# Twelve-layer fp32 network on one core: gate and up products under one 512-column operand, stage ends in token halves

## The chip, the cores and the metric

The kernel runs on one core of a Trainium2 chip. The metric is the device time of one execution in microseconds (us); the median of three runs before the change is 2283.48 us.

## The reference

Two networks follow each other on x of 256 tokens by 1024 features, all in float32. Each layer is a mixer or an FFN between two RMS norms:

```python
x = x + _rms(m, g[1])                                    # m: conv, pool or attention mixer of _rms(x, g[0])
f = _swiglu(_rms(x, g[2]), ffn_w_gate[i], ffn_w_up[i], ffn_w_down[i])
x = x + _rms(f, g[3])
def _swiglu(xn, w_gate, w_up, w_down):
    return (jax.nn.silu(xn @ w_gate) * (xn @ w_up)) @ w_down
```

There are eight FFNs with a hidden width of 2816, two convolution mixers, one pooling mixer, one differential attention and two mixers of dilated attention beside an mLSTM: 14 stages, in the order conv, ffn, pool, ffn, attn, ffn, conv, ffn, ffn, mix, ffn, ffn, mix, ffn.

## The kernel before

**Products.** Every float32 product is made of three products of parts in the type float32r: high times high, high times low, low times high (`three`, L483 to L487). Weights arrive in units of 1 MB (128 partitions by 2048 values), 349 in all, by the queue of SyncE into a ring of six buffers `raw`. ScalarE (ACT) copies a unit to its high part `w_hi` (L954, ring of four), VectorE (DVE) subtracts to get the low part `w_lo` (L1284, ring of six, in the place of `raw`). ACT may overwrite a high part once the unit four before is used (`unit_used`), and SyncE issues a load once the unit six before is used. `split(u)` is this step on ACT and on DVE, and `advance(to)` does all splits below `to` that are not done yet; its place in an engine's program sets when the split is made, since each engine works its list in order.

**An FFN stage** has 33 units: 11 steps of a gate unit, an up unit (256 hidden columns each) and an output unit. A gate or up unit is a `feature_unit`: the weights are stationary, the normed rows, transposed and split (`xT_hi`, `xT_lo`, 256 tokens), move, 48 matmuls of 256 columns. The first two units of a stage are made in token halves instead (`token_half`: 24 matmuls of 256 columns for 128 tokens, the rows stationary and the weights moving), so that half 0 can start before half 1 is normed; their product is turned by four transposes (`product_columns`). ACT applies Silu, DVE multiplies (`h_full`), ACT and DVE split the product into `h_hi` and `h_lo`, and the output unit adds 24 matmuls of 512 columns to four PSUM banks, two per token half. Steps 2 to 9 run in a hardware loop of two turns on each engine. The last two output units of a stage are ordered so that half 0 is finished first (`last_units`).

**A stage end** (the main loop over stages in the scalar and vector programs) is, for each token half h: squares of the sums (ACT, L982), 1/rms (POOL, L1764 to L1769), Y = sums times gain (DVE, L1725), X = Y * rstd + X (DVE, L1738), squares of X (ACT, L982), 1/rms (POOL), Y = X times gain (DVE, L1300), then times rstd (DVE, L1304), eight transposes on TensorE (`transpose_rows`, L576), the high part by ACT (`transposed`), the low part by DVE (L1312). Half 1's transposes stand after the first token half of the next stage (`first_units`). ACT and DVE do the splits up to unit `end` + 1 (`advance(end + 2)`, `end` is the first unit of the next stage) before the stage end begins. At the end of stage 0, DVE also copies `bias_row`, and POOL then writes it to DRAM 128 times over (L1847).

Of the kernel before, what the change touches and what calls it, by code (L numbers as in the profile page):

```python
# [38 lines left out]
HI_RING = 4  # L39
FFN_STEPS = FF // W  # L40
LOOP_STEPS = 4
TURNS = (FFN_STEPS - 3) // LOOP_STEPS
TURN = 3 * LOOP_STEPS
# [114 lines left out]
def build(nc, a, tab_at, tables, out, only=None):  # L158
# [25 lines left out]
    with ctx:  # L184
# [14 lines left out]
        xT_hi = sb("xT_hi", [P, KC, S], F32R)  # L199
        xT_lo = sb("xT_lo", [P, KC, S], F32R)  # L200
# [14 lines left out]
        with ExitStack() as g:  # L215
# [9 lines left out]
            bias_row = sb("bias_row", [4, 2 * S], scope=g)  # L225
        with ExitStack() as g:
# [111 lines left out]
        in_read = sem("in_read")  # L338
        gate_ready = sem("gate_ready")
        prod_ready = sem("prod_ready")  # L340
# [53 lines left out]
        def _(sp):  # L394
            def load(u, source, it=None):

                if u >= LO_RING:
                    v = u - LO_RING + 1
                    sp.wait_ge(unit_used, v if it is None else it * TURN + v)
                dst = raw[u % LO_RING][:].rearrange("p (c n) -> p c n", c=source.shape[1])  # L400
                sp.dma_start(dst, source).then_inc(raw_loaded[u % LO_RING], 16)
# [16 lines left out]
            for st in stages:  # L418
                u = st["u0"]
                if st["kind"] == "ffn":  # L420
                    w_gate, w_up, w_down, up0 = ffn_sources(st)

                    def block_in(u, i, it=None):

                        for n, (w, c) in enumerate(((w_gate, 0), (w_up, up0))):
                            c0 = c + i * W
                            c0 = c0 if it is None else it * (LOOP_STEPS * W) + c0
                            load(u + n, w[:, :, bass.ds(c0, W)], it)

                    def block_out(u, i, it=None):  # L430
                        r0 = i * W if it is None else it * (LOOP_STEPS * W) + i * W
                        load(u, chunks(w_down[bass.ds(r0, W), :]), it)
# [3 lines left out]
                    block_out(u + 4, 0)  # L436
                    with sp.Fori(0, TURNS) as it:
                        for b in range(LOOP_STEPS):
                            block_in(u + 5 + 3 * b, 2 + b, it)
                            block_out(u + 7 + 3 * b, 1 + b, it)  # L440
                    block_in(u + 29, FFN_STEPS - 1)
                    block_out(u + 31, FFN_STEPS - 2)
                    block_out(u + 32, FFN_STEPS - 1)
                elif st["kind"] == "conv":
                    ia = st["layer"] // 3
                    w_in, w_out = chunks(a["conv_w_in"][ia]), a["conv_w_out"][ia]
                    for i in range(D // W):
# [5 lines left out]
                        if i:  # L453
                            load(u, chunks(w_out[(i - 1) * W:i * W, :]))
                            u += 1
                    load(u, chunks(w_out[D - W:, :]))
# [23 lines left out]
        def _(pe):  # L480
# [8 lines left out]
            def unit_there(u, k, it=None):  # L489

                pe.wait_ge(lo_ready, u + 1 if it is None else it * TURN + (u + 1))
                return [w.rearrange("p (k n) -> p k n", k=k) for w in (w_hi[u % HI_RING][:], w_lo[u % LO_RING][:])]

            def feature_unit(u, b, it=None):
                hi, lo = unit_there(u, KC, it)
# [7 lines left out]
            def token_half(u, b, h):  # L503
# [3 lines left out]
                for k in range(KC):  # L507
                    mm = three(pair(b)[:, h, :], xT_hi[:, k, rows], xT_lo[:, k, rows],
# [26 lines left out]
            def product_columns():  # L535

                pe.wait_ge(prod_ready, seen.next(prod_ready))
                for c in range(2):
                    for h in range(H):
                        mm = pe.transpose(pair(4)[:, c, h * P:(h + 1) * P], prod[:, h, c * P:(c + 1) * P], ident[:])  # L540
                mm.then_inc(prodT_done, 1)

            def out_half(u, x_hi, x_lo, h, first, last, it=None):

                hi, lo = unit_there(u, 2, it)
# [11 lines left out]
            def out_unit(u, x_hi, x_lo, first, it=None):  # L557
                out_half(u, x_hi, x_lo, 0, first, False, it)
                out_half(u, x_hi, x_lo, 1, first, False, it).then_inc(unit_used, 1)

            def last_units(u, xs, before_last=None):

                out_half(u, *xs[0], 0, False, False)
                if before_last is not None:
                    pe.wait_ge(before_last, seen.next(before_last))
                out_half(u + 1, *xs[1], 0, False, True).then_inc(acc_done, 1)
                out_half(u, *xs[0], 1, False, False).then_inc(unit_used, 1)
                out_half(u + 1, *xs[1], 1, False, True).then_inc(unit_used, 1)

            def transpose_rows(h):  # L570

                for b in range(2):
                    pe.wait_ge(xn_ready, seen.next(xn_ready))
                    for j in range(4):
                        k = 4 * b + j
                        mm = pe.transpose(bank(4 + 2 * h + b)[:, j * P:(j + 1) * P],  # L576
# [3 lines left out]
            def ffn(u):  # L580
                base = seen.now(h_ready)

                def step_in(u, i, it=None):
                    for n in range(2):
                        feature_unit(u + n, 4 + 2 * (i % 2) + n, it)

                def step_out(u, i, it=None):
# [1294 lines left out]
```

## Time and profile before

| | |
|---|---|
| timed runs, median of 3 | 2283.48 us (2283.34 to 2283.98) |
| profiled execution, from its first to its last instruction | 2282.2 us |
| TensorE busy | 2183.5 us (96%), 15124 matmuls |
| VectorE busy | 1277.5 us (56%) |
| ScalarE busy | 992.4 us (43%) |
| mean granted clock of TensorE | 0.980 |

The page gives no time of the profiled execution other than this span. A busy time counts an instruction from its start to its end, overlaps only once; matmuls are pipelined, so the distance between two starts, not the duration of one, tells what one costs in a stream.

### The profile page before, as it was taken

To read this page: it belongs to the slowest core of one execution; us is meant where nothing else is said; L and a number is where in the kernel's file an instruction comes from. 1 tells how busy PE (TensorE), PEld (TensorE's weight loads), DVE (VectorE), ACT (ScalarE), POOL (GpSimd) and SP (SyncE) were. 2 spreads that over 40 slices of the span, in tenths; PEclk is the share of its full clock that TensorE was granted. 3 is DMA by queue.
4 is the path that set the end of the run, shared out by engine and by line. 5 is a ranking of instruction groups with operands and counts; after the bars stand their busy time and mean duration, and the time that the engine had idled before them with its cause. 6 is when DMAs were issued, how large, how long until landed. Compare 5 with 4: busy or idle time off the path is not lost.

```text
span 2282.2 us, 35632 instructions
## 1 busy us (share of the span) xinstructions
PE 2183.5 (96%) x15124; PEld 2027.6 (89%) x15124; DVE 1277.5 (56%) x1340; ACT 992.4 (43%) x1074; POOL 118.0 (5%) x231
## 2 busy tenths in 40 slices
PE   7969988999989999999999999989999999998998
PEld 7869978998979998899989989879998998887998
DVE  5645455445565457645464556775455545777454
ACT  4433444434554344344343444654344334455433
POOL 0000011001010000100020010010002001001000
PEclk9989999999999999999999999999999999999999
DMA  7556546555446555555565553236556555424552
GB/s 253 185 142 213 187 158 183 185 184 185 148 134 199 184 185 183 177 176 185 185 215 186 185 184 125 88 122 199 184 184 217 185 184 166 130 75 157 185 184 92
DMA packets 288662, 392.43 MB, mean 172 GB/s; under 512 B 7512, under 2 KB 255112, under 8 KB 288416
## 3 DMA queue, kind: packets, MB, share of 16 engines
q1 hardware_dynamic: 280928, 368.21, 49.6%
q10 hardware_dynamic: 4032, 14.68, 2.0%
q0 software_dynamic: 3584, 7.84, 1.6%
q8 instruction: 89, 1.46, 0.3%
q14 instruction: 29, 0.24, 0.0%
HBM read 388.60 MB, written 2.10 MB: 171 GB/s over the span
## 4 chain that ended last, share of the span: by engine, by line
PE 88%; DVE 5%; DMA 2%; ACT 2%; POOL 2%; issue 1%; POOLq 0%; DVEq 0%; SPq 0%; ACTq 0%
PE psum L485 28%; PE psum L487 27%; PE psum L486 27%; DMA raw<-in_ffn_w_up 2%; ACT squares L982 1%; POOL mean L1764 1%; DVE w_lo L1284 1%; DVE Y L1725 1%; DVE xT_lo L1312 1%; POOL rstd L1769 1%; DVE Y L1304 1%; DVE X L1738 1%; PE psum L841 1%; PE psum L869 1%; PE psum L576 1%
## 5 line engine op out<-in xcount | busy, mean ns | idle before, releaser
L485 PE MATMUL psum<-xT_hi,w_hi 128*128 128x256 f32 x3264 | 931.8, 285 | 16.2 <-DVE w_lo L1284 14.9
L486 PE MATMUL psum<-xT_lo,w_hi 128*128 128x256 f32 x3264 | 926.1, 284 | 0.0
L487 PE MATMUL psum<-xT_hi,w_lo 128*128 128x256 f32 x3264 | 925.9, 284 | 0.0
L1284 DVE TENSOR_TENSOR w_lo<-raw,w_hi 128x2048 fp32r<-128x2048 f32 x349 | 784.9, 2288 | 206.4 <-ACT w_hi L954 205.8
L954 ACT ACTIVATE w_hi<-raw 128x2048 fp32r<-128x2048 f32 x349 | 656.9, 1907 | 76.2 <-PE psum L487 46.2
L485 PEld LDWEIGHTS psum<-xT_hi,w_hi 128*128 128x128 f32 x3264 | 623.9, 191 | 26.0 <-DVE w_lo L1284 15.1
L486 PEld LDWEIGHTS psum<-xT_lo,w_hi 128*128 128x128 f32 x3264 | 623.9, 191 | 4.4 <-issue 1.0
L487 PEld LDWEIGHTS psum<-xT_hi,w_lo 128*128 128x128 f32 x3264 | 623.9, 191 | 0.0
L1347 DVE TENSOR_TENSOR h_full<-gate,psum 128x512 f32<-128x512 f32 x80 | 55.1, 688 | 471.1 <-PE psum L487 471.1
L487 PE MATMUL psum<-w_hi,h_lo 128*128 128x512 f32 x768 | 302.0, 393 | 0.0
L485 PE MATMUL psum<-w_hi,h_hi 128*128 128x512 f32 x768 | 300.3, 391 | 0.0
L486 PE MATMUL psum<-w_lo,h_hi 128*128 128x512 f32 x768 | 299.9, 391 | 0.0
L954 ACT ACTIVATE h_hi<-h_full 128x512 fp32r<-128x512 f32 x88 | 55.6, 632 | 493.8 <-DVE h_full L1347 441.9
L485 PE MATMUL psum<-w_hi,xT_hi 128*128 128x256 f32 (+1 forms) x688 | 219.3, 319 | 36.3 <-DVE xT_lo L1312 23.8
L486 PE MATMUL psum<-w_lo,xT_hi 128*128 128x256 f32 (+1 forms) x688 | 213.3, 310 | 0.0
L487 PE MATMUL psum<-w_hi,xT_lo 128*128 128x256 f32 (+1 forms) x688 | 212.8, 309 | 0.0
L485 PEld LDWEIGHTS psum<-w_hi,xT_hi 128*128 128x128 f32 x688 | 139.7, 203 | 50.1 <-DVE xT_lo L1312 26.7
L1003 ACT ACTIVATE gate<-psum 128x512 f32<-128x512 f32 x88 | 52.5, 596 | 292.1 <-PE psum L487 292.1
L487 PEld LDWEIGHTS psum<-w_hi,h_lo 128*128 128x128 f32 x768 | 144.3, 188 | 31.2
L486 PEld LDWEIGHTS psum<-w_lo,h_hi 128*128 128x128 f32 x768 | 144.2, 188 | 29.4
L485 PEld LDWEIGHTS psum<-w_hi,h_hi 128*128 128x128 f32 x768 | 144.4, 188 | 27.5
L487 PEld LDWEIGHTS psum<-w_hi,xT_lo 128*128 128x128 f32 x688 | 139.9, 203 | 4.1
(214 smaller groups left out, 1341.3 us busy)
## 6 DMA issues: line engine op xcount, KB each, us to landing
raw<-in_ffn_w_in SPq DMA_DIRECT2D x88, 1024.0 KB, 5.1
raw<-in_ffn_w_gate SPq DMA_DIRECT2D x44, 1024.0 KB, 5.3
raw<-in_ffn_w_up SPq DMA_DIRECT2D x44, 1024.0 KB, 5.3
raw<-in_ffn_w_down SPq DMA_DIRECT2D x44, 1024.0 KB, 4.9
raw<-in_ffn_w_out SPq DMA_DIRECT2D x44, 1024.0 KB, 4.9
raw<-in_mix_w_in SPq DMA_DIRECT2D x28, 1024.0 KB, 5.3
raw<-in_conv_w_in SPq DMA_DIRECT2D x24, 1024.0 KB, 5.2
raw<-in_attn_w_qkv SPq DMA_DIRECT2D x12, 1024.0 KB, 5.2
```

The lines of the kernel that those rows point to most:

```text
L485: pe.matmul(dst, l_hi, r_hi, start=first, stop=False, skip_group_check=loose)
L486: pe.matmul(dst, l_hi, r_lo, start=False, stop=False, skip_group_check=loose)
L487: return pe.matmul(dst, l_lo, r_hi, start=False, stop=last, skip_group_check=loose)
L576: mm = pe.transpose(bank(4 + 2 * h + b)[:, j * P:(j + 1) * P], Y[:, h, k * P:(k + 1) * P], ident[:])
L841: mm = pe.matmul(pair(0)[:, h, :], aqk[r, hd // 2, h * P:(h + 1) * P], aqk[r, 4 + hd // 2, :], start=True, stop=True)
L869: mm = pe.matmul(psum[r0:r0 + 64, 2 if hd < 6 else 5, 0:S], av[:, k, hd * 64:(hd + 1) * 64], a_probT[hd % 2][:, k, :], start=k == 0, stop= ...
L954: return act.activation(dst, source, ACT.Copy, **kw)
L982: act.activation(squares[:, 0:source.shape[1]], source, ACT.Square, scale=1.0 / 32, accum_out=ssum[:, col:col + 1]).then_inc(ss_ready, 1)
L1003: act.activation(gate[:], pair(4 + 2 * (i % 2)), ACT.Silu).then_inc(gate_ready, 1)
L1284: dve.tensor_tensor(w_lo[u % LO_RING][:], raw[u % LO_RING][:], f32(w_hi[u % HI_RING][:]), ALU.subtract).then_inc(lo_ready, 1)
L1304: dve.tensor_scalar(Y[:, h, c], Y[:, h, c], rstd[:, 2 + h:3 + h], None, ALU.mult).then_inc(xn_ready, 1)
L1347: dve.tensor_tensor(h_full[:], gate[:], pair(5 + 2 * (i % 2)), ALU.mult).then_inc(full_ready, 1)
```

## The change

1. `xT_hi` and `xT_lo` lie side by side in one tensor `xT`. In steps 2 to 10 of an FFN a gate or up unit is a `stacked_unit`: for each weight block, the high part meets high and low rows at once (512 columns, one whole PSUM bank), the low part meets the high rows (256 columns, added to the first half of the bank). The sum of the bank's two halves is the result: ACT copies the low half to SBUF, DVE adds the high half.
2. Steps 0 and 1 of an FFN are both in token halves, four units, each product turned by transposes. The output unit of step i stands after the gate and up units of step i + 2; the last three output units of an FFN, and of a convolution, are made half 0 first. There are four buffers of `h_hi` and `h_lo` instead of two. The hardware loops are gone.
3. The normed rows are made in one pass, from X, rstd and gain. Transposes go to PSUM banks 0 to 3, half 0's are served before half 1's sums, and a first product waits for half of the rows at a time.
4. The splits at a stage end stand elsewhere: `advance(end + 1)` ahead of it, the next after half 0, and two more within half 1.

```diff
+            def stacked_unit(u, b):
+                hi, lo = unit_there(u, KC)
+                for c in range(2):
+                    cols = slice(c * P, (c + 1) * P)
+                    for k in range(KC):
+                        pe.matmul(pair(b + c), hi[:, k, cols], xT[:, k, :, :], start=k == 0, stop=False)
+                        mm = pe.matmul(pair(b + c)[:, 0, :], lo[:, k, cols], xT_hi[:, k, :],
+                                       start=False, stop=k == KC - 1)
+                mm.then_inc(unit_used, 1)
...
             def first_units(u, b):
-                pe.wait_ge(xt_ready, seen.next(xt_ready, 2))
-                token_half(u, b, 0)
+                token_half(u, b, 0, rows_come=True)
+                token_half(u + 1, b + 1, 0)
                 transpose_rows(1)
-                token_half(u + 1, b + 1, 0)
-                pe.wait_ge(xt_ready, seen.next(xt_ready, 2))
-                token_half(u, b, 1).then_inc(unit_used, 1)
+                token_half(u, b, 1, rows_come=True).then_inc(unit_used, 1)
                 token_half(u + 1, b + 1, 1).then_inc(unit_used, 1)
...
+            def last_units(u, xs, made=None):
+                last = len(xs) - 1
+                for h in range(H):
+                    for n, x in enumerate(xs):
+                        if made is not None and h == 0:
+                            pe.wait_ge(made, seen.next(made))
+                        mm = out_half(u + n, *x, h, False, n == last)
...
             def ffn(u):                                   # TensorE
+                for n, b in enumerate((6, 7, 4, 5)):
+                    if n == 3:
+                        transpose_rows(1)
+                    token_half(u + n, b, 0, rows_come=n == 0)
+                for n, b in enumerate((6, 7, 4, 5)):
+                    if n == 3:
+                        pe.wait_ge(gate_taken, seen.next(gate_taken))
+                        product_columns(0)
+                    token_half(u + n, b, 1, rows_come=n == 0).then_inc(unit_used, 1)
+                for i in range(2, FFN_STEPS):
+                    step_in(u + 3 * i - 2, i)             # two stacked units, banks 6, 7 and 4, 5
+                    if i < FFN_STEPS - 1:
+                        step_out(u + 3 * i, i - 2)
+                last_units(u + 30, [(h_hi[i % H_BUFFERS], h_lo[i % H_BUFFERS])
+                                    for i in range(FFN_STEPS - 3, FFN_STEPS)], h_ready)
...
             def ffn(st):                                  # VectorE, steps 2 to 10
+                    dve.wait_ge(gate_low, seen.next(gate_low))
+                    dve.tensor_tensor(gate[:], psum[:, 6:8, 0:S], gate[:], ALU.add).then_inc(gate_taken, 1)
+                    advance(g + 5)
+                    dve.wait_ge(up_low, seen.next(up_low))
+                    dve.tensor_tensor(h_full[:], psum[:, 4:6, 0:S], h_full[:], ALU.add).then_inc(up_taken, 1)
+                    dve.wait_ge(up_taken, seen.next(up_taken))
+                    dve.wait_ge(gate_ready, seen.next(gate_ready))
+                    dve.tensor_tensor(h_full[:], h_full[:], gate[:], ALU.mult).then_inc(full_ready, 1)
+                    advance(g + 6)
+                    low_of_h(i, h_full[:])
...
             def normed_rows(h):
-                link(dve.tensor_tensor(Y[:, h, :], X[:, h, :], gain_pre[:], ALU.mult))
                 dve.wait_ge(rstd_ready, seen.next(rstd_ready))
                 for b in range(2):
                     c = slice(b * 512, (b + 1) * 512)
-                    dve.tensor_scalar(Y[:, h, c], Y[:, h, c], rstd[:, 2 + h:3 + h], None,
-                                      ALU.mult).then_inc(xn_ready, 1)
+                    dve.scalar_tensor_tensor(out=Y[:, h, c], in0=X[:, h, c], scalar=rstd[:, 2 + h:3 + h],
+                                             in1=gain_pre[:, c], op0=ALU.mult, op1=ALU.mult).then_inc(xn_ready, 1)
...
                 # the stage end, ScalarE
-                advance(end + 2)
+                advance(end + 1)
                 for h in range(H):
                     for b in range(2):
+                        if (h, b) == (1, 0 if st["kind"] == "pool" else 1) and new is not None:
+                            if new["kind"] != "pool":
+                                transposed(0)
...
                         square_sum(bank(2 * h + b), h + 4 * b)
+                    if h == 1:
+                        advance(end + 3)
                     if new is not None:
-                        if h == 1 and new["kind"] != "pool":
-                            transposed(0)
                         for b in range(2):
                             act.wait_ge(x_ready, seen.next(x_ready))
                             square_sum(X[:, h, b * 512:(b + 1) * 512], 2 + h + 4 * b)
+                    advance(end + 2 if h == 0 else end + 4)
...
                 # the stage end, VectorE
                     link(ins)                             # Y of half h
-                    if h == 1 and new is not None and new["kind"] != "pool":
-                        transposed(0)
+                    if h == 1:
+                        advance(end + 3)
...
                     dve.wait_ge(x_ready, seen.next(x_ready, 2))
                     if new is not None:
                         seen.skip(ss_ready, 2)
+                        if h == 1:
+                            advance(end + 4)
                         normed_rows(h)
-                if new is not None and new["kind"] != "pool":
-                    transposed(1)
+                        if new["kind"] != "pool":
+                            transposed(h)
+                    if h == 0:
+                        advance(end + 2)
```

In the convolution, the output units of steps 1 to 3 move behind all input units (`CONV_FIRST` gives each step's first unit), and ACT and DVE take two splits between the last gate product and the last `h_full`, two more after it.

## Rows read from the trace of the kernel before

**Rows 1.** The page, part 1: busy us (share of the span) x instructions.
```profile
PE 2183.5 (96%) x15124; PEld 2027.6 (89%) x15124; DVE 1277.5 (56%) x1340; ACT 992.4 (43%) x1074; POOL 118.0 (5%) x231
```
**Rows 2.** Groups by form, whole span: count, busy us, mean ns, idle before.
```profile
L1284 DVE TENSOR_TENSOR w_lo<-raw,w_hi 128x2048 fp32r<-128x2048 f32 x349 | 784.9, 2288 | 206.4 <-ACT w_hi L954 205.8
L954 ACT ACTIVATE w_hi<-raw 128x2048 fp32r<-128x2048 f32 x349 | 656.9, 1907 | 76.2 <-PE psum L487 46.2 <-DMA raw<-in_ffn_w_up 20.4 <-DMA raw<-in_ffn_w_gate 4.7
```
**Rows 3.** Stretch inside an FFN: from:to, us, busy by engine, PEclk, DMA share, GB/s.
```profile
1173.00:1349.00 176.00, 176.00 (x1232) 165.21 (x1232) 90.67 (x59) 73.36 (x63) 2.74 (x5) 1.00 0.57 187
```
**Rows 4.** Timeline of PE, first of 12 and first and last of 45 matmuls: start, us.
```profile
699.66 0.39 PE L485 MATMUL psum<-w_hi,h_hi 128*128 128x512 f32 x1
...
702.41 0.28 PE L485 MATMUL psum<-xT_hi,w_hi 128*128 128x256 f32 x1
...
707.69 0.28 PE L487 MATMUL psum<-xT_hi,w_lo 128*128 128x256 f32 x1
```
**Rows 5.** Timeline of PE at two stage ends.
```profile
1349.34 0.40 PE L487 MATMUL psum<-w_hi,h_lo 128*128 128x512 f32 x1
...
1358.33 0.36 PE L485 MATMUL psum<-w_hi,xT_hi 128*128 128x256 f32 x1
...
1716.71 0.40 PE L487 MATMUL psum<-w_hi,h_lo 128*128 128x512 f32 x1
1718.10 1.09 PE L576 MATMUL psum<-ident,Y 128*128 128x128 f32 x8 [0.99 <-DVE Y L1304]
1721.02 0.43 PE L485 MATMUL psum<-w_hi,xT_hi 128*128 128x256 f32 x1 [1.83 <-DVE xT_lo L1312]
...
1726.32 0.36 PE L485 MATMUL psum<-w_hi,xT_hi 128*128 128x256 f32 x1
```
**Rows 6.** Timeline of DVE at the second of these stage ends.
```profile
1709.40 2.29 DVE L1284 TENSOR_TENSOR w_lo<-raw,w_hi 128x2048 fp32r<-128x2048 f32 x1 [1.11 <-ACT w_hi L954]
...
1717.56 0.89 DVE L1304 TENSOR_SCALAR Y<-Y,rstd 128x512 f32<-128x512 f32 x2 [1.10 <-POOL rstd L1769]
1718.37 1.27 DVE L1725 SCALAR_TENSOR_TENSOR Y<-psum,gain_post 128x512 f32<-128x512 f32 x2
1719.67 1.29 DVE L1312 TENSOR_TENSOR xT_lo<-psum,xT_hi 128x512 fp32r<-128x512 f32 x2
1720.88 1.41 DVE L1738 SCALAR_TENSOR_TENSOR X<-Y,rstd,X 128x512 f32<-128x512 f32 x2
...
1724.65 1.20 DVE L1304 TENSOR_SCALAR Y<-Y,rstd 128x512 f32<-128x512 f32 x2 [1.11 <-POOL rstd L1769]
```
**Rows 7.** Timeline of ACT at the same stage end.
```profile
1711.64 0.60 ACT L982 ACTIVATE squares<-psum 128x512 f32<-128x512 f32 x1 [0.69 <-PE psum L487]
...
1718.79 1.08 ACT L954 ACTIVATE xT_hi<-psum 128x512 fp32r<-128x512 f32 x2 [0.96 <-PE psum L576]
...
1723.01 0.19 ACT L982 ACTIVATION_READ_ACCUMULATOR squares<-X 128x1 f32 x1
```
**Rows 8.** Timeline of DVE, end of the first convolution.
```profile
101.14 0.69 DVE L1399 TENSOR_TENSOR h_full<-conv_a,psum 128x512 f32<-128x512 f32 x1 [0.19 <-PE psum L487]
```
**Rows 9.** Stretches: the wait before the pool; 24 products at three clocks.
```profile
1721.02:1725.60 4.58, 4.58 (x26) 4.58 (x27) 3.44 (x5) 1.45 (x4) 2.97 (x4) 0.63 0.53 168
1159.52:1162.65 3.13, 3.13 (x24) 2.92 (x24) 2.49 (x3) 1.45 (x4) 1.53 (x3) 1.00 0.55 186
117.90:123.40 5.50, 5.50 (x26) 5.50 (x27) 3.85 (x5) 1.45 (x4) 3.17 (x4) 0.50 0.32 98
...
325.90:333.00 7.10, 0.06 (x2) 0.06 (x1) 5.78 (x10) 3.93 (x7) 2.93 (x7) 0.69 0.91 323
```
**Rows 10.** POOL's timeline, and the chain of waits around its write.
```profile
121.36 1.30 POOL L1847 DMA_DIRECT2D bias_scratch<-bias_row  x1
165.87 0.56 POOL L1776 DMA_DIRECT2D windows<-tables  x1 [43.21 <-DMA bias_scratch<-bias_row]
...
130.29 36.51 DMA raw<-in_ffn_w_up
```

More of the change, by code:

```diff
@@ L555, in out_half, with out_unit @@
                 return mm
[L557 to L568, printed above, removed]
+            def out_unit(u, x_hi, x_lo, first):
+                out_half(u, x_hi, x_lo, 0, first, False)
+                out_half(u, x_hi, x_lo, 1, first, False).then_inc(unit_used, 1)
+            def last_units(u, xs, made=None):
[6 more added lines that the diff above has]
+                        if h == 1:
+                            mm.then_inc(unit_used, 1)
+                        elif n == last:
+                            mm.then_inc(acc_done, 1)
             def transpose_rows(h):
@@ L580, in ffn @@
             def ffn(u):
[L581 to L587, printed above, removed]
-                    pe.wait_ge(h_ready, base + i + 1 if it is None else it * LOOP_STEPS + (base + i + 1))
-                    out_unit(u, h_hi[i % 2], h_lo[i % 2], it is None and i == 0, it)
-                first_units(u, 4)
-                feature_unit(u + 2, 6)
@@ L1014, in ffn @@
-                step(0)
-                step(1)
-                with act.Fori(0, TURNS) as it:
-                    for b in range(LOOP_STEPS):
-                        step(2 + b, it)
-                cursor[0] += 3 * (FFN_STEPS - 3)
-                step(FFN_STEPS - 1)
-                seen.skip(full_ready, FFN_STEPS - 1)
+                advance(u + 4)
+                for i, b in ((0, 6), (1, 4)):
+                    result_of(u + 2 * i)
+                    act.activation(gate[:], pair(b), ACT.Silu).then_inc(gate_ready, 1)
+                    advance(u + 2 * i + 5)
+                    act.wait_ge(prodT_done, seen.next(prodT_done))
+                    copy(h_hi[i][:], pair(i)).then_inc(hh_ready, 1)
+                    advance(u + 2 * i + 6)
@@ new lines, in ffn @@
+                for i in range(2, FFN_STEPS):
+                    g = u + 3 * i - 2
+                    result_of(g)
+                    copy(gate[:], psum[:, 6:8, S:2 * S]).then_inc(gate_low, 1)
+                    advance(g + 5)
+                    act.wait_ge(gate_taken, seen.next(gate_taken, 2 if i == 2 else 1))
+                    act.activation(gate[:], gate[:], ACT.Silu).then_inc(gate_ready, 1)
+                    result_of(g + 1)
+                    act.wait_ge(h_ready, seen.next(h_ready, 2 if i == 2 else 1))
+                    copy(h_full[:], psum[:, 4:6, S:2 * S]).then_inc(up_low, 1)
+                    advance(g + 6)
+                    act.wait_ge(full_ready, seen.next(full_ready))
+                    copy(h_hi[i % H_BUFFERS][:], h_full[:]).then_inc(hh_ready, 1)
+                    if i < FFN_STEPS - 1:
+                        advance(g + 7)
@@ L1023, in conv @@
+                seen.skip(h_ready, 1)
             def conv(st):
@@ L1350, in ffn @@
[L1350 to L1358 removed]
+                advance(u + 4)
+                for i, (b, taken) in enumerate(((7, gate_taken), (5, up_taken))):
+                    dve.wait_ge(gate_ready, seen.next(gate_ready))
+                    result_of(u + 2 * i + 1)
+                    dve.tensor_tensor(prod[:], gate[:], pair(b), ALU.mult).then_inc(taken, 1)
+                    seen.skip(taken, 1)
+                    advance(u + 2 * i + 5)
+                    low_of_h(i, pair(i))
+                    advance(u + 2 * i + 6)
```

238 lines of the change are left out of this document (100 added, 138 removed).

## The prediction

> **What bounds the kernel now.** I read the page first: TensorE (PE) is busy 2183.5 us of a span of 2282.2 us, VectorE (DVE) 56% and ScalarE (ACT) 43% [rows 1]. The timed median is 2283.48 us, 1.3 us above the span; all sums below are made against the span, and the 1.3 us is added again at the end. Then the groups by form: each of the 349 weight units costs ACT 1.91 us (high part) and DVE 2.29 us (low part) [rows 2]. Then the stretches: inside an FFN PE is busy 176.00 us of 176.00 [rows 3], with two turns of the hardware loop in it. So inside a stage only the number and length of matmuls counts, and DVE and ACT have room. PE's free time lies at the stage ends, and there the reader should see a chain through DVE, ACT and POOL. These two places move in opposite directions in this change.
>
> **The stacked units.** Before, a gate or up unit is 48 matmuls of 256 columns; 44 starts lie between 702.41 and 707.69 us, 0.120 us each. The 512-column starts before them go from 699.66 to 702.41 us in 12 steps, 0.229 us each [rows 4]. After, 16 groups of one 512 and one 256: 0.229 + 0.120 = 0.349 instead of 0.360 us, 0.011 us a group, 0.175 us a unit. Nine steps times two units times eight FFNs are 144 units; two of them fall before the 15 us stall of the first FFN (below) and are absorbed. 142 x 0.175 = -24.8 us. From both sides: 256 columns at 2.4 GHz are 0.107 us, so the two pitches hold a fixed part of 0.013 and 0.015 us, and the gain is that one part less per group. A 512-column pitch of 0.236 instead of 0.229 would halve it, one of 0.225 would make it -34 us; and if the mixed order of 512 and 256 columns costs what it saves, it is 0. I take the rows' value.
>
> [...]
>
> **What the FFN pays inside.** Four more product transposes per FFN at 0.11 us (8 in 1.09 us, [rows 5]): 0.45 x 7 = +3.1 us, the first FFN's hidden in its stall. The extra ACT copies (0.6 us, two per step) and DVE adds (0.69 us, two per step) [rows 2, 6]: per step of 16.7 us DVE then has 3 x 2.29 + 4 x 0.69 = 9.6 us and ACT about 8.2 us. The gate banks are free within 7 us of the gate unit, and PE has 11 us of other work first (up unit and output unit): no wait. At the end the last h: up unit done, ACT copy 0.6, add and product 1.4, the next unit's split (2.29, waits for ACT's 1.9 until 2.5), low part 0.69: about 5.8 us, PE has two halves of 2.75 = 5.5 us. +0.3 x 7 = 2.1 us. Removing the loops: 0, since PE does not pause at a turn [rows 3]. The Trainium skill, "Runtime: NRT & Kernel Launch", section "Instruction fetch mechanics", says a taken branch to a page outside the window waits for a fetch. By that the unrolling would give something at 16 turns; the row with 176.00 busy of 176.00 leaves nothing for it here.
>
> **The stage end, step by step.** Take E as the moment PE is free after the last output product: last start 1716.71 + 0.23 = 1716.94 [rows 5]. Before: transposes of half 0 at 1718.10, first product of the next stage 1721.02, then one token half, the transposes of half 1, and the next token half at 1726.32: 9.38 us for one half of 24 x 0.12 = 2.88 us, so 6.5 us are lost. At a boundary that keeps its clock it is 1358.33 - (1349.34 + 0.23) - 2.88 = 5.9 [rows 5]. I take 6.3.
>
> After, FFN to FFN. Three output units run in halves, so PE works 8.2 us after half 0's sums are done, where it worked 5.5. The chain to the normed rows took 1711.64 to 1717.56 = 5.9 us [rows 6, 7], now 6.7 with the first pass of 0.75 us. It is hidden: transposes at E. ACT takes them at +0.7 (1718.79 - 1718.10), DVE's first low half is ready at +2.0, and PE starts there instead of at +4.1. That is the gain of the edit. But DVE's queue now holds this, in order: both low halves until +2.6; split of unit end+1, 2.29, to +4.9; Y of half 1, 1.28, to +6.2; split end+2 to +8.6; X, 1.41, to +10.0; split end+3, whose high part ACT makes only after the squares of X (done 2.3 us after X starts [rows 6, 7], +10.9, plus 1.9 = +12.8), so to +15.1; normed rows 1, first half +15.9, second +16.6. Before, the splits of end and end+1 were done ahead of E (1709.40 is the last) and that of end+2 after it all: from 1717.56 to the second normed row DVE has no split [rows 6]. PE does three halves (the third waits for split end+2 at +8.6) to +11.5, then waits: transposes to +17.1. Loss 17.1 - 3 x 2.88 = 8.4 us. Against 6.3: +2.1, twice = +4.2.
>
> The rest by the same walk. FFN to attention, convolution and mix (four): only two halves stand before the transposes, and half 1 needs its low parts: PE goes on at +18.0, loss 12.2, +5.9 each = +23.6. Attention and mix to FFN (three): last_units still has two units, so half 0's chain ends at +1.0, not before E; everything 1.2 us later, loss 9.7, +3.4 each = +10.2. Convolution to FFN (stage 6): 8.4, and its third output half waits 2.4 us for split 15, which DVE makes after h_lo of the last step (before, with one split less, DVE came to the last product 0.19 us ahead of PE [rows 8]; now a second split of 2.29 stands there); before it lost 8.6: +2.2. FFN to pool: before 7.1 us [rows 9], after the same DVE queue without transposes gives 13.4: +6.3. Pool to FFN: transposes of half 0 are served 2.4 us earlier, then two splits: +3.3. Sum +49.8 us.
>
> **Stage 0 and the scratch write.** POOL's write of the bias table is issued at 121.36 and lands at 165.87; a weight load issued at 130.29 lands with it, 36.5 us later, and PE stands 15 us [rows 10]. The write starts when bias_row is copied and half 1 is normed: 9.4 us after E before, 13.1 after; E itself is 1.8 us later (2.4 of the convolution's wait, 0.6 gained at the start). The stall ends with the write: +5.5 us. It swallows the rest of that boundary.
>
> **The clock.** PE's granted clock falls to half (1.2 GHz) after many of these ends: 24 products took 4.6 us at 0.63 and 3.1 at 1.00 [rows 9]. Before, this was mostly hidden, as half 1's chain ended later anyway. After, it follows the long wait in front of the transposes (4.5 to 8 us) and falls on products that nothing hides: 1.5 us each, 12 ends, three quarters of them: +14 us (bounds 0 and, at the 5.5 us that the same 24 products took at 0.50, 12 x 2.4 = 29 [rows 9]).
>
> **Sum:** -24.8 + 3.1 + 2.1 + 49.8 + 5.5 + 14 = +49.7; 2282.2 + 49.7 + 1.3 = **2333 us**, slower by 2.2%.
>
> **Rivals.** (1) The splits do not hold the chain of half 1. It decides if the wait in front of the second transposes stays under 3 us: then the ends gain 1.7 us each from the earlier start and the stacking counts in full. -24.8 + 5.2 - 13 x 1.7 = -42: 2242 us, faster. For it: ACT and DVE are idle half the time. Against: in-order queues, and three splits of 2.29 us in front of the normed rows are more than PE's 8.6 us of halves can cover, with 4 us of other DVE work. The change is faster wherever the ends cost less than 1.5 us each on average. 14%. (2) The stacking gives nothing, the pair costs 0.360 us as before, since the fixed part goes with the change of width and not with the matmul: 2333 + 25 = 2358 us. For it: the gain rests on a small difference, 0.011 us, and no row has a 512 behind a 256 with the same weights' order. Against: the step from 512 to 256 columns at 702.41 shows no extra time [rows 4]. 10%. [...] (3) The ends lengthen, but half the predicted amount (DVE gets to split end+1 before E, or ACT's part overlaps), clock undisturbed: -19.6 + 28 = 2292 us. 14%. The forecast has 62%.
>
> **Range and chances.** A kernel of this spread can't be told from no change within 0.2% (4.6 us). The forecast's own range is 2310 to 2365 (stack -34 to 0, clock 0 to 29). With rivals 2 and 3: 2286 to 2368. Faster 0.15 (rival 1, and a sliver of 3), same 0.04, slower 0.81.
>
> **What would show it.** Right: FFN interiors with a pitch of 0.349 us per pair and 16.65 us a step instead of 17.0; a first product 2 us after E; then a wait of PE for normed rows of 4 to 8 us, with three splits on DVE in the 15 us after E; a convolution with a 2.4 us wait before its last output unit; the 15 us stall still there, 5 us later. Wrong: DVE reaching the normed rows of half 1 before E + 12, or a pair at 0.36 us.

## The result, and the profile after

The kernel after the change takes 2333.17 us (median of four runs, 2332.67 to 2337.31), beside 2283.73 us for the kernel before on the same chip: a ratio of 1.0214 (1.0199 to 1.0228). It is slower by 2.1%, and 2333 us had been forecast. The profiled span grew from 2282.2 to 2330.9 us, by 48.7 us. From the page after, the span, part 1, and two of the groups of part 5:

```profile
span 2330.9 us, 30203 instructions
...
PE 2186.1 (94%) x12852; PEld 1916.4 (82%) x12852; DVE 1359.6 (58%) x1456; ACT 1062.7 (46%) x1218; POOL 106.7 (5%) x231
...
L510 PE MATMUL psum<-xT,w_hi 128*128 128x512 f32 x2304 | 815.7, 398 | 1.2 <-DVE gate L1356 1.2
L511 PE MATMUL psum<-xT,w_lo 128*128 128x256 f32 x2304 | 646.6, 281 | 0.0
```

Beside [rows 1], PE has 2272 instructions fewer and 2.6 us more busy time. A busy PE at the lower clock counts as busy too, and that share has grown, so the saving is not to be seen here. PE's free time grew from 98.7 to 144.8 us, by 46.1.

Inside an FFN the forecast holds. A stretch of the FFN after, with the columns of [rows 3], and five products of a stacked unit:

```profile
1205.00:1370.00 165.00, 165.00 (x890) 141.68 (x890) 96.63 (x73) 78.28 (x74) 0.98 (x3) 1.00 0.58 191
```
```profile
1265.95 0.40 PE L510 MATMUL psum<-xT,w_hi 128*128 128x512 f32 x1
1266.19 0.28 PE L511 MATMUL psum<-xT,w_lo 128*128 128x256 f32 x1
1266.31 0.40 PE L510 MATMUL psum<-xT,w_hi 128*128 128x512 f32 x1
1266.54 0.28 PE L511 MATMUL psum<-xT,w_lo 128*128 128x256 f32 x1
1266.66 0.40 PE L510 MATMUL psum<-xT,w_hi 128*128 128x512 f32 x1
```

PE is never without work: the extra copies and additions on ACT and DVE are hidden. Two pairs take 1266.66 - 1265.95 = 0.71 us; over a unit the mean is 0.236 + 0.1165 = 0.3525 us a pair, where 0.349 was forecast and 0.360 is what three products of 256 columns take. A step of the FFN fell from 17.01 to 16.76 us.

The stage ends are where the time went. The end between the two FFNs of stages 7 and 8: E, the moment the last output product is done, is 1180.23 + 0.23 = 1180.46. PE first, and then DVE's whole list from there:

```profile
1180.23 0.39 PE L488 MATMUL psum<-w_hi,h_lo 128*128 128x512 f32 x1
1180.46 1.03 PE L591 MATMUL psum<-ident,Y 128*128 128x128 f32 x8
1182.56 0.36 PE L486 MATMUL psum<-w_hi,xT 128*128 128x256 f32 x1 [1.07 <-DVE xT L1333]
...
1195.91 1.74 PE L591 MATMUL psum<-ident,Y 128*128 128x128 f32 x8 [3.97 <-DVE Y L1325]
1197.30 0.56 PE L486 MATMUL psum<-w_hi,xT 128*128 128x256 f32 x1
```
```profile
1181.72 1.29 DVE L1333 TENSOR_TENSOR xT<-psum,xT 128x512 fp32r<-128x512 f32 x2 [2.64 <-ACT xT L977]
1182.93 2.30 DVE L1306 TENSOR_TENSOR w_lo<-raw,w_hi 128x2048 fp32r<-128x2048 f32 x1
1185.16 1.27 DVE L1734 SCALAR_TENSOR_TENSOR Y<-psum,gain_post 128x512 f32<-128x512 f32 x2
1186.47 2.29 DVE L1306 TENSOR_TENSOR w_lo<-raw,w_hi 128x2048 fp32r<-128x2048 f32 x1
1188.68 1.41 DVE L1747 SCALAR_TENSOR_TENSOR X<-Y,rstd,X 128x512 f32<-128x512 f32 x2
1192.90 2.29 DVE L1306 TENSOR_TENSOR w_lo<-raw,w_hi 128x2048 fp32r<-128x2048 f32 x1 [2.81 <-ACT w_hi L977]
1195.11 1.41 DVE L1325 SCALAR_TENSOR_TENSOR Y<-X,rstd,gain_pre 128x512 f32<-128x512 f32 x2
```

Before, PE went on 4.1 us after E at the end of [rows 5], and 3.7 us after it at this one; now 2.1 us after, so the edit gains what it should. But where DVE before had no split between its two normed rows [rows 6], three splits now stand in front of half 1's. The third waits 2.81 us for its high part, which ACT makes only behind the squares. The normed rows start at E + 14.65, and PE stands 3.97 us and has its next product at E + 16.84. Where only two halves stand before the transposes, as at the end from FFN to mix (E = 1375.95), the wait is longer, and the next product comes at E + 18.06:

```profile
1391.39 1.97 PE L591 MATMUL psum<-ident,Y 128*128 128x128 f32 x8 [7.35 <-DVE Y L1325]
1394.01 0.56 PE L486 MATMUL psum<-w_hi,xT 128*128 128x256 f32 x1 [0.65 <-DVE xT L1333]
```

The same transposes take 1.03 us at E and 1.97 us here: the clock has fallen. The stretch that begins with them, and then the 18 us from E on:

```profile
1391.00:1400.00 9.00, 7.96 (x43) 7.59 (x44) 2.81 (x6) 1.79 (x3) 0.00 (x0) 0.61 0.18 59
```
```profile
1376.00:1394.00 18.00, 8.95 (x65) 8.15 (x64) 12.63 (x12) 7.91 (x12) 3.85 (x10) 0.83 0.41 132
```

From E on PE is busy for half the time, 8.95 of 18.00 us, at a mean clock of 0.83; in the stretch behind it the mean is 0.61. Added up over the span of the trace, PE is granted the lower of its two clocks for 89.9 us before and for 130.7 us after. It is busy in 66.2 us of the first and in 88.9 us of the second; the rest falls into its free time and costs nothing.

### The profile page after: what moved, and what is told of

Read it like the earlier page. It is cut to its first block, busy times and chain, and to the rows that moved or that the text cites. A ratio compares the mean times of both kernels' runs of the same rounds, so it can differ in the third digit from the quotient of the medians.

```text
span 2330.9 us, 30203 instructions
## 1 busy us (share of the span) xinstructions
PE 2186.1 (94%) x12852; PEld 1916.4 (82%) x12852; DVE 1359.6 (58%) x1456; ACT 1062.7 (46%) x1218; POOL 106.7 (5%) x231
## 4 chain that ended last, share of the span: by engine, by line
PE 84%; DVE 9%; ACT 3%; DMA 2%; issue 1%; POOL 0%; ACTq 0%; POOLq 0%; DVEq 0%; SPq 0%
PE psum L510 23%; PE psum L486 15%; PE psum L487 15%; PE psum L488 15%; PE psum L511 12%; DVE w_lo L1306 4%; ACT w_hi L977 1%; DMA raw<-in_ffn_w_gate 1%; PE psum L591 1%; ACT squares L1003 1%; DVE xT L1333 1%; DVE Y L1734 1%; ACT xT L977 1%; PE psum L864 1%; DVE X L1747 1%
## 5 line engine op out<-in xcount | busy, mean ns | idle before, releaser
L1306 DVE TENSOR_TENSOR w_lo<-raw,w_hi 128x2048 fp32r<-128x2048 f32 x349 | 798.4, 2290 | 363.0 <-ACT w_hi L977 362.4
L510 PE MATMUL psum<-xT,w_hi 128*128 128x512 f32 x2304 | 815.7, 398 | 1.2 <-DVE gate L1356 1.2
L511 PE MATMUL psum<-xT,w_lo 128*128 128x256 f32 x2304 | 646.6, 281 | 0.0
L510 PEld LDWEIGHTS psum<-xT,w_hi 128*128 128x128 f32 x2304 | 432.7, 188 | 106.4 <-DVE gate L1356 1.7
L511 PEld LDWEIGHTS psum<-xT,w_lo 128*128 128x128 f32 x2304 | 435.2, 189 | 2.6
L486 PE MATMUL psum<-w_hi,xT 128*128 128x256 f32 (+1 forms) x944 | 294.6, 312 | 36.1 <-DVE xT L1333 16.3
L487 PE MATMUL psum<-w_lo,xT 128*128 128x256 f32 (+1 forms) x944 | 286.8, 304 | 0.0
L488 PE MATMUL psum<-w_hi,xT 128*128 128x256 f32 (+1 forms) x944 | 286.3, 303 | 0.0
L486 PEld LDWEIGHTS psum<-w_hi,xT 128*128 128x128 f32 x944 | 191.0, 202 | 52.5 <-issue 29.0
L486 PE MATMUL psum<-xT,w_hi 128*128 128x256 f32 x704 | 205.6, 292 | 1.4 <-ACT u_pad L977 1.4
L487 PE MATMUL psum<-xT,w_hi 128*128 128x256 f32 x704 | 200.9, 285 | 0.0
L488 PE MATMUL psum<-xT,w_lo 128*128 128x256 f32 x704 | 200.7, 285 | 0.0
L487 PEld LDWEIGHTS psum<-w_lo,xT 128*128 128x128 f32 x944 | 190.8, 202 | 3.7
L488 PEld LDWEIGHTS psum<-w_hi,xT 128*128 128x128 f32 x944 | 190.1, 201 | 4.0
```

The costliest lines, as they stand in the source:

```text
L486: pe.matmul(dst, l_hi, r_hi, start=first, stop=False, skip_group_check=loose)
L487: pe.matmul(dst, l_hi, r_lo, start=False, stop=False, skip_group_check=loose)
L488: return pe.matmul(dst, l_lo, r_hi, start=False, stop=last, skip_group_check=loose)
L510: pe.matmul(pair(b + c), hi[:, k, cols], xT[:, k, :, :], start=k == 0, stop=False)
L511: mm = pe.matmul(pair(b + c)[:, 0, :], lo[:, k, cols], xT_hi[:, k, :], start=False, stop=k == KC - 1)
L1306: dve.tensor_tensor(w_lo[u % LO_RING][:], raw[u % LO_RING][:], f32(w_hi[u % HI_RING][:]), ALU.subtract).then_inc(lo_ready, 1)
```

## The experiments

Each is compared with the kernel before on its own chip, whose median lay between 2283.7 and 2284.6 us. "Half clock" is the time within the span for which the trace grants PE 1.2 GHz, and behind it how much of that time PE is busy; "free" is the time in which PE has no work.

| kernel | us | ratio (interval) | half clock, of it busy | free |
|---|---|---|---|---|
| before | 2283.73 | 1 | 89.9, 66.2 | 98.7 |
| after | 2333.17 | 1.0214 (1.0199 to 1.0228) | 130.7, 88.9 | 144.8 |
| e1, pairs of 256 | 2352.45 | 1.0298 (1.0281 to 1.0315) | 150.2, 104.5 | 141.7 |
| e2, last split behind the rows | 2306.03 | 1.0096 (1.0079 to 1.0113) | 100.5, 78.5 | 120.7 |
| e3, all splits in idle time | 2261.88 | 0.9903 (0.9886 to 0.9919) | 65.2, 50.1 | 92.7 |
| e4, e3 and the convolution's order | 2256.85 | 0.9882 (0.9866 to 0.9899) | 66.9, 51.5 | 88.5 |
| e5, before with the moved splits | 2397.88 | 1.0499 (1.0482 to 1.0517) | 199.4, 137.9 | 178.7 |
| e6, e4 and the table by way of DRAM | 2241.27 | 0.9813 (0.9797 to 0.983) | 48.1, 37.5 | 78.9 |
| e7, after with rows in two passes | 2346.58 | 1.0278 (1.0261 to 1.0295) | 145.3, 97.0 | 154.7 |
| e8, before with e6's table | 2267.24 | 0.9931 (0.9915 to 0.9948) | 78.9, 66.7 | 81.8 |
| e9, after with the low product first | 2323.72 | 1.0176 (1.0159 to 1.0193) | 126.2, 83.7 | 145.4 |
| e10, e6 and e9's order | 2248.48 | 0.9837 (0.982 to 0.9853) | 79.8, 71.0 | 79.1 |

What the half clock costs is an estimate: half of the time in which PE is busy at it. With PE's free time this accounts for the two largest steps: from before to e5 80.0 + 35.9 = 116 us where 114 were measured, and from after to e3 52.1 + 19.4 = 71.5 where 71.3 were.

**e1: what is the wide operand worth?** The 512-column product is issued as two of 256. All columns are still computed, only by three matmuls a block instead of two. The kernel stands for its time alone: its sums are not the reference's.

```diff
-pe.matmul(pair(b + c), hi[:, k, cols], xT[:, k, :, :], start=k == 0, stop=False)
+pe.matmul(pair(b + c)[:, 0, :], hi[:, k, cols], xT_hi[:, k, :], start=k == 0, stop=False)
+pe.matmul(pair(b + c)[:, 1, :], hi[:, k, cols], xT_lo[:, k, :], start=k == 0,
+          stop=k == KC - 1, skip_group_check=True)
```

> The changed kernel, with each 512-column product of a stacked unit issued as two of 256 columns into the same two halves of the bank; all else as changed. What the stacked operand itself is worth. My forecast took 0.175 us a unit from the pitches before (0.229 + 0.120 against 0.360): 142 units, +25 us, 2358 us. The changed kernel's own trace shows 0.236 + 0.1165 = 0.3525 us a pair, so if three starts cost 0.360 again it is 16 x 0.0075 = 0.12 us a unit: +17 us, 2350 us. If the second matmul with the same stationary block is cheaper than one with a new block (no fixed part), nothing: 2333 us.

It took 19.3 us more than after. PE's timeline of it:

```profile
1265.86 0.28 PE L510 MATMUL psum<-xT,w_hi 128*128 128x256 f32 x1
1265.98 0.28 PE L511 MATMUL psum<-xT,w_hi 128*128 128x256 f32 x1
1266.10 0.28 PE L513 MATMUL psum<-xT,w_lo 128*128 128x256 f32 x1
1266.22 0.28 PE L510 MATMUL psum<-xT,w_hi 128*128 128x256 f32 x1
```

Three products take 0.360 us, as before the change. Stacking is worth some 18 us (71 steps by 0.25), so rival 2 falls, and so does the full 25. The forecast of 2350 us from the pair of 0.3525 came within 2.5 us.

**e2 and e3: do the splits' places make the loss?** In e2 the last split of a stage end (end + 3) goes behind half 1's normed rows; in e3 every split goes where DVE otherwise waits: end + 1 behind half 0's rows, end + 2 behind half 1's X, end + 3 behind half 1's rows. In both, the last split stands ahead of half 1's low parts before an FFN and behind them before the other stages. e2, VectorE's program:

```diff
+                        normed_rows(h)
+                        if h == 1 and new["kind"] == "ffn":
+                            advance(end + 4)
+                        if new["kind"] != "pool":
+                            transposed(h)
                         if h == 1:
                             advance(end + 4)
-                        normed_rows(h)
-                        if new["kind"] != "pool":
-                            transposed(h)
```

and e3:

```diff
                     link(ins)                             # Y of half h
-                    if h == 1:
-                        advance(end + 3)
...
                         if h == 1:
+                            advance(end + 3)
+                        normed_rows(h)
+                        if h == 1 and new["kind"] == "ffn":
                             advance(end + 4)
-                        normed_rows(h)
+                        if h == 0:
+                            advance(end + 2)
                         if new["kind"] != "pool":
                             transposed(h)
-                    if h == 0:
-                        advance(end + 2)
+                        if h == 1:
+                            advance(end + 4)
```

> The changed kernel, with one edit at a stage end on VectorE: the split of unit end+3 stands behind the normed rows of half 1 (before an FFN) or behind half 1's low parts (before other stages), not ahead of the rows. Theory (VectorE's in-order queue holds the rows back): rows at E+12.3 instead of E+15.2. Before an FFN the fourth token half then waits for that split instead (E+16.1 against 17.1, -1.0 each, eight ends), before the other stages half 1 goes on at E+15.2 against 18.0 (-2.9 each, four ends), the pool -2.8: about -21 us, 2312 us. Rival (the wait comes from the squares and POOL, the split only fills it): no change, 2333 us.

> The changed kernel, with all three splits of a stage end moved on VectorE: end+1 behind half 0's normed rows and ahead of its low parts (VectorE idles there), end+2 behind X of half 1 where it waits for the squares and POOL, end+3 behind the rows. Work and all other engines' programs are the same. Theory: rows of half 1 at E+7.8 to 8.6. Loss at an end before an FFN 2.9 instead of 8.4 us, before attention, convolution and mix 4.9 instead of 12.2, behind attention and mix 6 less, around the pool 5 less each: 74 us in sum, and some 10 us of slow clock with it: 2249 us, below the kernel before. Rival (1) of the prediction would have had the ends hide the splits in any place: then no change, 2333 us. If only the number of splits inside the end counts and not their place, no change either.

e2 is 27.1 us faster than after: one split of 2.29 us at 13 ends. e3 is 71.3 us faster, and beats the kernel before. DVE in e3 at the same end as above, from stage 7 to stage 8, with E = 1147.66:

```profile
1146.21 2.28 DVE L1306 TENSOR_TENSOR w_lo<-raw,w_hi 128x2048 fp32r<-128x2048 f32 x1
1148.93 1.29 DVE L1333 TENSOR_TENSOR xT<-psum,xT 128x512 fp32r<-128x512 f32 x2 [0.43 <-ACT xT L977]
1150.13 1.28 DVE L1734 SCALAR_TENSOR_TENSOR Y<-psum,gain_post 128x512 f32<-128x512 f32 x2
1151.45 1.41 DVE L1745 SCALAR_TENSOR_TENSOR X<-Y,rstd,X 128x512 f32<-128x512 f32 x2
1152.89 2.29 DVE L1306 TENSOR_TENSOR w_lo<-raw,w_hi 128x2048 fp32r<-128x2048 f32 x1
1156.22 1.41 DVE L1325 SCALAR_TENSOR_TENSOR Y<-X,rstd,gain_pre 128x512 f32<-128x512 f32 x2 [1.04 <-POOL rstd L1784]
1157.56 2.28 DVE L1306 TENSOR_TENSOR w_lo<-raw,w_hi 128x2048 fp32r<-128x2048 f32 x1
```

The same three splits are there. One begins while PE still makes the last output products, one while ACT and POOL make half 1's 1/rms (even behind it, DVE waits 1.04 us for POOL), one behind the rows. The rows start at E + 8.56 instead of E + 14.65. Expected were 84 us, 74 of them at the ends and 10 by the clock. PE's free time fell by 52.1 us and its busy time at half clock by 38.8, an estimated 19. So the ends gave less than expected and the clock more. Here the next product came at E + 12.2, a loss of 3.6 us and not 2.9; the most is missing behind attention and mix, where the free time of the next stage fell by 2.9 us each (5.8 to 2.9) and not by 6.

**e5: the moved splits alone, in the kernel before.** Only the four places of `advance` at a stage end are those of the change; 256-column products, loops and two-pass rows stay. One thing differs from the change: there half 0's low parts come ahead of the split of end + 1, here behind it, as the kernel before makes them later. VectorE's program (ScalarE's changes alike):

```diff
-                advance(end + 2)
+                advance(end + 1)
...
+                    if h == 1:
+                        advance(end + 3)
...
+                        if h == 1:
+                            advance(end + 4)
                         normed_rows(h)
+                    if h == 0:
+                        advance(end + 2)
```

> The kernel before, with only the places of the splits at a stage end as in the changed kernel (one less ahead of it, end+1 after half 0, end+2 after half 0's low parts, end+3 ahead of half 1's rows). Operands, units, order of the output units and the two passes stay. Theory: this alone makes it slower: low parts of half 0 at E+6.4 instead of 4.0, rows of half 1 at E+16.9, the second token half at E+17.9 instead of 9.4; about +8.7 us at ten ends, +10 around the pool, +15 of slow clock: 2395 us. Rival (the units in token halves and the other order of PE's work make the ends longer, not the splits): 2283 us, within 10 us.

It is slower by 114 us, where 111 had been expected. PE at the same end, E = 1208.88:

```profile
1209.71 1.09 PE L576 MATMUL psum<-ident,Y 128*128 128x128 f32 x8 [0.66 <-DVE Y L1307]
1214.83 0.58 PE L485 MATMUL psum<-w_hi,xT_hi 128*128 128x256 f32 x1 [4.02 <-DVE xT_lo L1315]
...
1225.24 1.97 PE L576 MATMUL psum<-ident,Y 128*128 128x128 f32 x8 [4.99 <-DVE Y L1307]
```

The first product comes at E + 5.9 instead of the 3.7 of the kernel before, and half 1's transposes stand at E + 16.4 behind a wait of 4.99 us. So in the old order of work the places of the splits alone cost more than the whole change, and the rest of the change takes part of it back: with the splits out of the way (e3) that rest is a gain.

**e7: the one-pass rows.** After, with the gain multiplied in a pass of its own, as before.

```diff
+link(dve.tensor_tensor(Y[:, h, :], X[:, h, :], gain_pre[:], ALU.mult))
 dve.wait_ge(rstd_ready, seen.next(rstd_ready))
-dve.scalar_tensor_tensor(out=Y[:, h, c], in0=X[:, h, c], scalar=rstd[:, 2 + h:3 + h], ...)
+dve.tensor_scalar(Y[:, h, c], Y[:, h, c], rstd[:, 2 + h:3 + h], None, ALU.mult)
```

> The changed kernel with the normed rows in two passes again (X times gain over 1024 columns, then times rstd). As the split of end+3 stands ahead of both, the first pass of 1.23 us no longer hides in the wait for POOL: rows come 1.0 us later for the first half and 0.75 for the second, at eleven ends that count: +8 us, 2341 us. Rival (the pass is hidden as it was before the change, and the second pass of 0.5 is shorter than the one pass of 0.75): 3 us faster, 2330 us.

13.4 us slower, where 8 had been expected: the product behind half 1's transposes comes 1.0 to 1.5 us later at ten ends, and 0.7 later before the pool. Behind the third split nothing hides the extra pass, which takes 1.22 us at the end from stage 7 to 8:

```profile
1200.01 1.22 DVE L1322 TENSOR_TENSOR Y<-X,gain_pre 128x1024 f32<-128x1024 f32 x1
```

**e4, e6, e8: the first two stages.** The end of stage 0 and PE's wait in stage 1, first in the kernel after, from the timelines of POOL, ACT and PE:

```profile
129.57 1.18 POOL L1860 DMA_DIRECT2D bias_scratch<-bias_row  x1
174.24 0.56 POOL L1789 DMA_DIRECT2D windows<-tables  x1 [43.50 <-DMA bias_scratch<-bias_row]
```
```profile
167.77 1.91 ACT L977 ACTIVATE w_hi<-raw 128x2048 fp32r<-128x2048 f32 x1 [14.37 <-DMA raw<-in_ffn_w_down]
```
```profile
172.66 0.79 PE L486 MATMUL psum<-w_hi,h_hi 128*128 128x512 f32 x1 [7.57 <-DVE h_lo L1340]
```

The write starts 8.2 us later than before [rows 10] and lasts as long, but the load that ACT waits for ends its wait at 167.77, 6.5 us before the write has landed. PE's wait is 7.6 us here, where it had been 15. In e4, ACT and DVE make the convolution's split 15 before the last h is split (one `advance(first + 6)` more in each program). In e6, besides, POOL writes the table to one row in DRAM, and the copy to 128 rows reads it from there:

```diff
-pool.dma_start(scratch[:, :, 0:2 * S], bias_row[:].unsqueeze(1).broadcast_to([4, P, 2 * S]))
+pool.dma_start(scratch_row[:, :], bias_row[:]).then_inc(scratch_stored, 16)
+pool.wait_ge(scratch_stored, seen.next(scratch_stored, 16))
+pool.dma_start(scratch[:, :, 0:2 * S], scratch_row[:, :].unsqueeze(1).broadcast_to([4, P, 2 * S]))
```

> The kernel of e3_splits_in_idle_time, and in the convolution's last step ScalarE makes the high part of the last output unit before it waits for h_full, VectorE the low part between h_full and h_lo. The wait ahead of the last output unit (2.25 us in both convolutions) should fall to 0.3 us. Theory: stage 6 gains 2 us, stage 0's share is swallowed by the stall of stage 1, whose end hangs on the scratch write: 2260 us. Rival (the stall moves with the start of the write, and the whole gain of stage 0 counts): 2258 us.

> The kernel of e4_conv_and_ends, and the bias table goes to DRAM once as four rows and is repeated from there 128 times by a second DMA from DRAM to DRAM, in place of one DMA that reads 4 partitions 128 times over (44 us). Theory (the write's packets hold the DMA engines on which the weight load queues): the write is some 10 us long, PE's two waits of 7.9 and 2.3 us in stage 1 and the slow clock behind them go: 2248 us. Rival (the loads are slow there for another reason, such as the gains' broadcast loads): 2260 us.

> The kernel before, with only the scratch write of e6_scratch_over_dram. It tells how much of that kernel's lead has nothing to do with the change. Theory (the 15 us wait of PE in stage 1 is the write alone): 2284 - 15 and 1.7 of slow clock behind it: 2267 us, so e6 keeps a lead of 26 us. Rival (a part of the wait is the load order of the stage, in which the loads come late anyway): some 2275 us.

e4 gained 5.0 us on e3 (its four runs spread from 2254.2 to 2260.7 us), and PE no longer waits ahead of a convolution's last output unit. e6 gained 15.6 us on e4. The broadcast now takes 18.8 us instead of 44 (some 10 had been expected), and PE waits for no load in stage 1:

```profile
125.67 1.17 POOL L1869 DMA_DIRECT2D bias_scratch<-bias_scratch_row  x1 [1.50 <-DMA bias_scratch_row<-bias_row]
144.45 0.57 POOL L1796 DMA_DIRECT2D windows<-tables  x1 [17.62 <-DMA bias_scratch<-bias_scratch_row]
```

In the kernel before, the same edit is worth 16.6 us (e8), and the wait of 15 us is gone. e6 is the fastest version: 1.9% faster than before, and 26 us faster than a kernel before with the same write.

**e9 and e10: the order inside a pair.** The 256-column product of a block goes in front of the next 512-column one (512, 256, 256, 512, 256, 512, ...).

> The changed kernel, with the two products of a stacked pair in the other order from the second block on (low weights with 256 columns first, then high weights with 512). The pair costs 0.236 + 0.1165 us in the changed kernel, where the pitches before were 0.229 and 0.120. Theory (each product waits a fixed part for its stationary block, whatever the order): the pair stays at 0.352 us and the time at 2333 us. Rival (a 512 behind a 256 is what costs the extra 7 ns, because 256 columns are too short to hide the next block's load): now the order inside the loop is the same alternation, so the pitch follows the neighbour, not the program order, and nothing moves either; a change by more than 3 us in either direction would say that the order of the sums in the bank matters.

> The kernel of e6_scratch_over_dram with the order of the products of e9_low_product_first. That order shortened an FFN step from 16.76 to 16.66 us in the trace and the changed kernel by 9 us. If it is a matter of the stacked unit alone it adds to the other edits: 72 steps by 0.10 us, 2234 us. If it came from what stands around the units at the ends, which e6 has altered, it is less: 2241 us.

e9 gained 9.4 us where neither the theory nor the rival expected anything. Its timeline:

```profile
1265.73 0.40 PE L513 MATMUL psum<-xT,w_hi 128*128 128x512 f32 x1
1265.96 0.28 PE L511 MATMUL psum<-xT,w_lo 128*128 128x256 f32 x1
1266.08 0.40 PE L513 MATMUL psum<-xT,w_hi 128*128 128x512 f32 x1
```

A pair took 0.350 us (0.234 + 0.116), a step 16.66 us, which is the forecast's value. That is 72 steps by 0.10 = 7.2 us; the rest is about what 5.2 us less of busy time at half clock make (88.9 to 83.7). Why the order matters is open. e10 puts it into e6, keeps the 16.66 us, and yet is 7.2 us slower than e6. The whole of stage 9, a mix, in e6 and then in e10:

```profile
1318.70:1487.60 168.90, 160.95 (x1077) 139.37 (x1075) 118.54 (x245) 86.55 (x126) 8.64 (x19) 0.99 0.37 120
```
```profile
1315.70:1490.90 175.20, 167.24 (x1077) 145.14 (x1075) 118.55 (x246) 86.66 (x126) 8.65 (x19) 0.95 0.36 115
```

The same 1077 matmuls take 6.3 us more of busy time at a clock of 0.95 instead of 0.99. Over the trace PE's free time is alike (78.9 and 79.1 us), but PE is busy at half clock for 71.0 us instead of 37.5; the two mix stages are 10.7 us longer, and the shorter steps give only a part of it back. Even one program varies: one of e10's four runs took 2243.17 us at a mean clock of 0.985, the others 2248.3 to 2249.4 us at 0.981 to 0.982. What makes the clock fall in one and not in the other was not found.

## Why the prediction was right, step by step

The mechanism was the one forecast, and rivals 1 and 3 fall with DVE's list above; e5 and e3 show from both sides that the splits in front of half 1's rows make the loss. The sum was right to about 1 us by luck as well: errors of size cancel. From E to E, with the forecast for each stage without its clock term, all in us:

| stages (number) | forecast | measured |
|---|---|---|
| conv and first FFN (0, 1) | +2.7 | +0.7 |
| pool, and the FFN after it (2, 3) | +6.3, +0.9 | +4.8, -2.3 |
| attention (4) | +5.9 | +8.2 |
| conv (6) | +8.3 | +10.5 |
| mix (9, 12) | +5.9 each | +5.1, +10.8 |
| FFN after attention or mix (5, 10, 13) | +1.0 each | +2.5, +2.8, +2.4 |
| FFN after conv or FFN (7, 8, 11) | -2.6, -0.3, -0.3 | +0.2, +1.7, +1.2 |
| sum | +35.7, with +14 for the clock +49.7 | +48.6 |

(A stage's forecast is the end before it, plus for an FFN 18 units by -0.175, +0.45 and +0.3, in the first FFN 16 units alone, and for stage 6 the 2.4 us of its last output unit, which the prediction had in its conv to FFN term.)

- **The stacked units**: mis-sized. The pair measured 0.3525 us and not 0.349; the gain is 18 us instead of 25. The term took the 512's pitch, the distance between two starts, from a stream of 512s [rows 4]. In the mixed order a 512 takes 0.236 us and not 0.229, which the text names as its other bound, and a 256 takes 0.1165 and not 0.120, which it does not; with 0.236 alone 9 us would be left of the 25. The Trainium skill, "TensorE: Matmul & The Clock Gate", section "Back-to-back issue gap", gives columns / 2.4 GHz + 2.5 ns for a single matmul by itself, about 216 ns at 512 columns, and 131 ns for a stream of weight loads and matmuls. This stream shows 229 to 236 ns, above both, and the measurement decides.
- **Inside the FFN**: right; PE without a gap of work in 165 us, and nothing to gain from the loops.
- **The stage ends but the pool's**: right within 0.7 us where read: next product at E + 16.84 (17.1 forecast), E + 18.06 (18.0), for attention and mix to FFN E + 18.08 and E + 17.64 (18.3). The convolution's last output unit came 2.0 us late (2.4).
- **The pool's two ends**: ahead of the pool right, PE's first product at E + 13.0 (13.4). Behind it "then two splits: +3.3" failed: DVE has one split, not two, between half 1's X and its rows, and between half 0's rows and that X only half 0's low parts and the pool's own work:

```profile
363.50 1.42 DVE L1747 SCALAR_TENSOR_TENSOR X<-pool_y,rstd,X 128x512 f32<-128x512 f32 x2 [1.12 <-POOL rstd L1782]
367.73 2.29 DVE L1306 TENSOR_TENSOR w_lo<-raw,w_hi 128x2048 fp32r<-128x2048 f32 x1 [2.82 <-ACT w_hi L977]
369.94 1.41 DVE L1325 SCALAR_TENSOR_TENSOR Y<-X,rstd,gain_pre 128x512 f32<-128x512 f32 x2
```

  PE goes on behind half 1's transposes 19.2 us after the pool's last product, with three halves between, and before it was 14.1 us with one: a loss of 10.5 instead of 11.2 us, so -0.7 and not +3.3.
- **The table's write**: "the stall ends with the write" failed. It took the one load of [rows 10] that landed together with the write for a rule. The write started 8.2 us later and not 5.5, since E of stage 0 came 4.5 us later and not 1.8. Yet the load that counts here was done 6.5 us before the write's end, and the two stages cost 0.7 us instead of 2.7.
- **The clock**: +14 forecast. PE is busy at half clock for 22.7 us more than before (66.2 to 88.9), an estimated 11 us. Where these fall no walk through the queues told: the two mix stages, 9 and 12, run the same code and cost +5.1 and +10.8 us. Their free time grew almost alike, by 5.5 and 6.6 us, but the busy time at half clock went from 13.7 to 12.8 us in the first and from 10.2 to 19.1 in the second, an estimated 5 us between them.
- **Cancelled**: stacking 7 too good; against it the pool's ends some 4.5, the clock some 3 and the write 2 too dear.
- **The range**: its lower end is the sum of its bounds (2333 - 9 - 14 = 2310), its upper end is not: 2333 + 25 + 15 is 2373, where 2365 stands.

## What to carry to other kernels

Where a chain crosses several in-order engines, list for each engine everything that stands in its queue between two links; work for later belongs where that engine waits anyway, and at these ends moving three splits of 2.29 us by one or two places turned +49 us into -22. Ahead of unrolling or widening products, measure the pitch in the mixed order, not in streams of one width: 4608 matmuls instead of 6912 were worth 18 us in 2300. A change that comes out slower can hold a gain: take apart what is bundled, and keep the parts that pay.

## What the runs showed that was not expected

- The order of products in a pair is worth 0.0025 us a pair, 0.10 us a step and 7 of the 9 us by which e9 is faster.
- Two programs that differ in that order alone (e6, e10), with the same free time, are busy at half clock for 37.5 and 71.0 us.
- A broadcast write of the same megabyte takes 44 us from SBUF and 18.8 us from four rows in DRAM, and PE waits for a weight load only beside the first (after and e6, before and e8).
